# Seven half-depth block products in place of eight in the feed-forward gate and up projection

## The reference, cut to what matters

```python
h = _rmsnorm(x, norm_ffn_pre[l]).astype(dt)          # 1024 x 1024
gate, up = jnp.split(h @ ffn_w_up[l], 2, axis=-1)    # 1024 x 5632 -> 2 x 2816
gate = _causal_dwconv(gate, ffn_conv_w[l], ffn_conv_b[l])   # 3 taps
f = jax.nn.gelu(gate, approximate=True) * up
x = x + _rmsnorm(f @ ffn_w_down[l], norm_ffn_post[l]).astype(dt)
```

## Time and profile before

| | before |
|---|---|
| median of three runs | 3194.17 us |
| profiled execution, from its first to its last instruction (its own time) | 3201.0 us |
| TensorE busy | 2841.4 us (89%) |
| VectorE / ScalarE / GpSimd busy | 1815.1 / 1345.1 / 350.6 us |
| mean granted TensorE clock | 0.928 |

### The profile page before, as it was taken

The page is one execution under the profiler, slowest core; times in us unless marked ns, Lnnn a source line. Parts: engine busy times, 40 slices in busy tenths (PEclk is TensorE's granted clock), DMA queues, the critical chain, the costliest instruction groups (busy, mean ns, idle before and its releaser), DMA issues. The chain is left out here.

```text
span 3201.0 us, 42557 instructions
## 1 busy us (share of the span) xinstructions
PE 2841.4 (89%) x14715; PEld 2372.3 (74%) x14715; DVE 1815.1 (57%) x2267; ACT 1345.1 (42%) x2039; POOL 350.6 (11%) x246
## 2 busy tenths in 40 slices
PE   5999987799689999994999978677787999999998
PEld 5888776687578888883877777566676888887886
DVE  3995517764479999995462447664445233333344
ACT  4122427613178888883322134663335222222233
POOL 1222210020011112112122101002000000000000
PEclk9999998899789999997999978787598999999999
DMA  3112225133199999995212210402022111110122
GB/s 101 33 50 79 83 90 180 40 125 127 58 390 414 414 415 414 417 413 196 69 54 80 74 44 2 133 1 54 7 105 87 52 52 46 46 52 26 46 87 103
DMA packets 247664, 421.10 MB, mean 132 GB/s; under 512 B 33581, under 2 KB 152404, under 8 KB 247540
## 3 DMA queue, kind: packets, MB, share of 16 engines
q1 hardware_dynamic: 218356, 349.89, 30.3%
q10 hardware_dynamic: 20336, 39.59, 3.3%
q0 software_dynamic: 8848, 29.96, 2.8%
HBM read 349.05 MB, written 70.33 MB: 131 GB/s over the span
## 5 line engine op out<-in xcount | busy, mean ns | idle before, releaser
L2181 DVE TENSOR_TENSOR e_w_lo<-e_ring,e_w_hi 128x1024 fp32r<-128x1024 f32 x384 | 446.6, 1217 | 46.6 <-ACT e_w_hi L2108 46.6
L2108 ACT CAST e_w_hi<-e_ring 128x1024 fp32r<-128x1024 f32 x384 | 377.2, 1049 | 35.3 <-PE banks L2041 28.5
L2476 PE MATMUL banks<-h_hi,u_w_hi 128*128 128x512 f32 x672 | 262.8, 391 | 4.7 <-DVE u_w_lo L2519 4.7
L2477 PE MATMUL banks<-h_lo,u_w_hi 128*128 128x512 f32 x672 | 262.4, 391 | 0.0
L2478 PE MATMUL banks<-h_hi,u_w_lo 128*128 128x512 f32 x672 | 262.4, 390 | 0.0
L2039 PE MATMUL banks<-e_w_hi,e_xT_hi 128*128 128x512 f32 x512 | 203.1, 397 | 0.0
L2041 PE MATMUL banks<-e_w_hi,e_xT_lo 128*128 128x512 f32 x512 | 200.1, 391 | 0.0
L2040 PE MATMUL banks<-e_w_lo,e_xT_hi 128*128 128x512 f32 x512 | 199.7, 390 | 0.0
L949 DVE SCALAR_TENSOR_TENSOR conv<-x_first,vectors,conv 128x1024 f32<-128x1024 f32 x120 | 187.3, 1561 | 9.8 <-issue 0.9
L2476 PEld LDWEIGHTS banks<-h_hi,u_w_hi 128*128 128x128 f32 x672 | 126.8, 189 | 31.5 <-DVE u_w_lo L2519 4.9
L2296 PE MATMUL banks<-fd_w_hi,fd_s_hi 128*128 128x512 f32 x352 | 139.1, 395 | 11.4 <-DVE fd_s_lo L2392 11.4
(11 more groups left out here) (598 smaller groups left out, 6782.3 us busy)
## 6 DMA issues: line engine op xcount, KB each, us to landing
e_ring<-in_w_gate_e_dram SPq DMA_DIRECT2D x128, 512.0 KB, 6.0
e_ring<-in_w_up_e_dram SPq DMA_DIRECT2D x128, 512.0 KB, 6.1
e_ring<-in_w_down_e_dram SPq DMA_DIRECT2D x128, 512.0 KB, 5.2
yT<-in_ffn_w_up_dram SPq DMA_DIRECT2D x44, 512.0 KB, 3.9
expert_results<-nothing SPq DMA_DIRECT2D x1, 16384.0 KB
expert_results<-e_y ACTq DMA_DIRECT2D x32, 512.0 KB, 7.6
p_w<-in_w_in_dram SPq DMA_DIRECT2D x24, 512.0 KB, 3.8
fd_w<-in_ffn_w_down_dram SPq DMA_DIRECT2D x42, 256.0 KB, 2.6
```

Of the source, the lines that this page charges most:

```text
L2108: nc.scalar.copy(w_hi[:, part, :], experts.ring[:, slot, :]).then_inc(w_rounded, 1)
L2181: tt(w_lo[:, part, :], experts.ring[:, slot, :], w_hi[:, part, :].bitcast(F32), ALU.subtract).then_inc(w_split, 1)
L2476: nc.tensor.matmul(bank, w_hi[:, up, k, :], h_hi[:, k, tokens], start=(k == 0), stop=False)
L2477: nc.tensor.matmul(bank, w_hi[:, up, k, :], h_lo[:, k, tokens], start=False, stop=False)
```

## The change: what it does

**Products.** For column tile j let the gate weights be two halves of depth G0, G1 and the up weights U0, U1 (512 x 128 each), and let the activations be split by depth half and by token half: a0, a1 for tokens 0 to 511, b0, b1 for tokens 512 to 1023. Gate and up columns of both token halves are a 2 x 2 by 2 x 2 block product. It is made with seven products of half depth (4 depth slices, 512 tokens, 3 parts, so 12 matmuls each: 84 a tile) and not eight (96). The products are numbered m = 1 to 7. Products 1, 2 and 3 take plain activation halves (`own_hi`, `own_lo`), 4 to 7 take sums of them (`sum_hi`, `sum_lo`, which lie as four pieces of 128 tokens). Products 1, 2 and 4 take plain weights, 7, 5, 6 and 3 take weight sums. Their order for a tile is 1, 7, 5, 6, 2, 4, 3, apart from the first two tiles.

**Weight sums.** GpSimd makes four sums or differences of 128 x 512 for each tile (`weight_sums`), in two buffers. ScalarE and VectorE round and split seven operands of 128 x 512 a tile through a ring of five (before: two of 128 x 1024).

**Activation sums.** Before the loop, for each u of four, `chain(u)` on GpSimd (three operations of 128 x 512), `cross(u)` on VectorE (one), `round_sums(u)` on ScalarE and `part_sums(u)` on VectorE (128 x 2048 each). The products 1 and 2 of the first two tiles stand before them on TensorE; the first sums are used in two halves of 256 tokens.

**Combining.** ScalarE copies product 1 and the first gate half out of PSUM (128 x 512 each). VectorE does six additions of 128 x 512 with one operand in PSUM, in two of which an intermediate is formed.

**Result.** `f` is no longer kept in SBUF during `ffn_up`. Tiles 0 and 1 stay in `xn`; SP stores tiles 2 to 21 to DRAM (512 KB each), and `fd` loads them back while it makes its first pass. `ffn_up` ends only when the last store has landed. All streams of `ffn_up` are written out, without hardware loops.

```diff
-            with sp.Fori(1, pairs) as i:
-                for b in range(2):
-                    load(i, b, 0, i * 2 + b)
+            if rows is None:
...
+                for i in range(1, pairs):
+                    for b in range(2):
+                        sp.wait_ge(split, 4 * i + 2 * b + 1)
+                        sp.dma_start(w[:, b, :], weight[0][(2 * i + b) * P:(2 * i + b + 1) * P, 0:HALF]).then_inc(landed[b], 16)
+                    if i == 1:
+                        load_rows(1)
+                    if i + 1 < pairs:
+                        load_rows(i + 1)
...
-def ffn_up(K, h_hi, h_lo, room, f, norm, first, x_stored):
+def ffn_up(K, x, sums, xn, first, rows, x_stored):
...
+    KH, NH, RING = KT // 2, NT // 2, 5
+    order = [(0, 1), (0, 2), (1, 1), (1, 2)] + [(j, m) for j in range(2) for m in (7, 5, 6, 4, 3)] \
+        + [(j, m) for j in range(2, FFT) for m in (1, 7, 5, 6, 2, 4, 3)]
...
+            def store(j):
+                sp.wait_ge(done, j + 1)
+                sp.dma_start(rows[j * P:(j + 1) * P, :], c).then_inc(stored, 16)
...
+            sp.wait_ge(stored, 16 * (FFT - 2))
...
+                for k in range(KH):
+                    hi, lo = right(0, m, k, q), right(1, m, k, q)
+                    place = out if m in OWN else out.rearrange("p (u n) -> p u n", n=P)
+                    mm(place, w_hi[:, n % RING, k, :], hi, start=opens and k == 0 and not q, stop=False, skip_group_check=True)
+                    mm(place, w_hi[:, n % RING, k, :], lo, start=False, stop=False, skip_group_check=True)
+                    last = mm(place, w_lo[:, n % RING, k, :], hi, start=False, stop=(k == KH - 1), skip_group_check=True)
...
+            for t in range(4):
+                turn(t)
+            for m in (1, 2):
+                for q in range(2):
+                    pe.wait_ge(own_parted, 2 * q + 2)
+                    product(0, m, q)
+                    turn(2 * m + 2 + q)
+            product(1, 1)
+            product(1, 2)
+            for q in range(2):
+                pe.wait_ge(sum_parted, 2 * q + 2)
+                for m in (7, 5, 6):
+                    product(0, m, q)
...
+            def weight_sums(j):
+                pool.wait_ge(landed[j % 2], 32 * (j // 2) + 32)
+                if j >= 2:
+                    pool.wait_ge(split, at[j - 2, 3] + 1)
+                gate, upper, out = w[:, j % 2, 0], w[:, j % 2, 1], w_sums[j % 2]
+                tt(out[:, 0], gate[:, 0:KH], upper[:, 0:KH], ALU.subtract).then_inc(summed, 1)
+                tt(out[:, 1], upper[:, 0:KH], upper[:, KH:KT], ALU.add).then_inc(summed, 1)
+                pool.drain()
+                tt(out[:, 2], out[:, 1], gate[:, 0:KH], ALU.subtract).then_inc(summed, 1)
+                pool.drain()
+                tt(out[:, 3], gate[:, KH:KT], out[:, 2], ALU.subtract).then_inc(summed, 1)
...
+            def chain(u):
...
+                tt(tile_of(u)[:, low], tile_of(t)[:, low], tile_of(u)[:, low], ALU.subtract).then_inc(chained, 1)
...
+                pool.wait_ge(crossed, u + 1)
+                tt(tile_of(t)[:, high], tile_of(t)[:, high], tile_of(u)[:, low], ALU.subtract)
+                pool.drain()
+                tt(tile_of(u)[:, high], tile_of(u)[:, high], tile_of(t)[:, high], ALU.subtract).then_inc(chained, 1)
...
+            def event(n):
+                j, m = order[n]
+                if m == 7:
+                    dve.wait_ge(made, n + 1)
+                    dve.wait_ge(copied, j + 1)
+                    tt(xy, bank(j, 7), first[:, j % 2, :], ALU.add).then_inc(x_taken, 1)
+                if m == 5:
...
+                    tt(xy, bank(j, 5), xy, ALU.add).then_inc(y_taken, 1)
+                if m == 6:
+                    if j >= 1:
+                        finish(j - 1)
...
+                    tt(v, bank(j, 6), first[:, j % 2, :], ALU.add)
+                    tt(up[:, HALF:S], bank(j, 6), xy, ALU.add).then_inc(b_taken, 1)
+                if m == 4:
...
+                    tt(up[:, 0:HALF], bank(j, 4), v, ALU.add).then_inc(c_taken, 1)
+                if m == 3:
+                    dve.wait_ge(made, n + 1)
+                    tt(g[:, 2 + HALF:2 + S], bank(j, 3), v, ALU.add).then_inc(d_taken, 1)
+                fill(n + RING)
+                if m == 3:
+                    convolve(j)
...
+            for u in range(NH):
+                part_own(NH + u)
+                cross(u)
+                part_sums(u)
+                fill(5 + u)
...
+            f_rows = K.dram("ffn_rows", (DFF, S))
```

More of the change, by code:

```diff
@@ L2227, in _, with project_and_add @@
                 split_w(*tail(used, j))
-def project_and_add(K, tag, srcT, depth, weight, gain_row, x, y, src, out, squares=False, first=None):
+def project_and_add(K, tag, srcT, depth, weight, gain_row, x, y, src, out, squares=False, first=None, rows=None, head=None):
     nc = K.nc
@@ L2246, in project_and_add @@
     pairs = depth // 2
+    row_landed = [K.sem(f"{tag}_row_landed{b}") for b in range(2)] if rows is not None else None
     own = 16 if first is None else 0
@@ L2459, in _, with load @@
[L2459 to L2464, removed]
+            def load(j):
+                for up_half in range(2):
+                    sp.dma_start(w[:, j % 2, up_half], w_up[:, :, up_half * DFF + j * P:up_half * DFF + (j + 1) * P]).then_inc(landed[j % 2], 16)
@@ L2465, in _ @@
             sp.wait_ge(fetched, 32)
+            sp.wait_ge(stored, 16 * (FFT - 2))
         @block.tensor
         def _(pe):
[L2469 to L2486, removed]
+            mm = nc.tensor.matmul
+            def turn(t):
+                b = t % 2
+                pe.wait_ge(scaled, t + 1)
+                if t >= 2:
+                    pe.wait_ge(gained, t - 1)
+                for k in range(KT):
+                    last = nc.tensor.transpose(K.ps[:, 4 + 2 * b + k // 4, (k % 4) * P:(k % 4 + 1) * P], xn[:, b, k * P:(k + 1) * P], K.const("ident"))
+                last.then_inc(turned, 1)
@@ L2507, in _ @@
             act.wait_ge(rated, 1)
[L2508 to L2513, removed]
+            scale(0)
+            scale(1)
+            fill(0)
+            for t in range(NH):
+                round_own(t)
+                scale(t + 2)
+                if t < 3:
+                    fill(t + 1)
@@ new lines, in _ @@
+            for u in range(2):
+                scale(u + NT - 2)
+                round_own(NH + u)
+            event(0)
+            fill(4)
+            round_sums(0)
+            round_own(NH + 2)
+            event(2)
+            fill(5)
+            round_sums(1)
+            round_own(NH + 3)
+            fill(6)
+            round_sums(2)
+            fill(7)
+            round_sums(3)
+            fill(8)
+            for n in range(at[0, 7], len(order)):
+                event(n)
+            gelu(FFT - 1)
```

289 lines of the change are left out of this document (230 added, 59 removed).

## The result

The changed kernel takes 3174.8 us (median of four runs, 3169.7 to 3182.9) against 3194.9 us (3190.0 to 3201.1): ratio 0.9932, 95% interval 0.9915 to 0.9949, so 16 to 27 us are gained, 20.1 by the medians. The forecast was 3167. The profiled execution, the fastest of the four, has a span of 3167.9 us (before: 3201.0). The forecast's span for it was 3173.

A forecast was written before the change was run, and what follows sets the result against it. TensorE was taken as the bound, by matmul count and spacing. Start -37.3, end +8.6 and spacing +1 gave -27.7 us: 3194.2 to 3166.5, forecast 3167, own range 3157 to 3183, 8 in 10 3155 to 3189.

The forecast's parts named there:

- Bound and spacing: In the loop, TensorE is the bound at 0.2265 us a matmul; a tile falls from 21.7 to 19.0 us.
- rival B: In the loop, matmuls with a moving operand in four pieces run slower; gain gone at 26 ns each; chance 0.06.
- VectorE in the loop: Per loop tile, VectorE needs 14 us plus 3 for GpSimd's disturbance: 17 us, at most 18.6, under TensorE's 19.0.
- The 88%: Share of GpSimd's time that VectorE lost in an unbroken stretch of taps, 8.5 of 9.6 us; here at most 4.5 a tile.
- Rival A: In the loop, VectorE becomes the bound: strong form 22.0 us a tile, 3227, chance 0.07; mild 20 us, 3187, chance 0.08.
- ScalarE: Per loop tile, ScalarE's roundings, copies, gelu and at most two table loads take 9.3 us.
- The start: From the first scaling until TensorE's stream is unbroken, the longer preparation eats 22.5 of 59.8 us, leaving a gain of 37.3.
- 2448: In the start, the time in us by which plain rests of the first four tiles would be done.
- tiles 4 to 7 ... 3.7 us each: In the start, these tiles go one by one through 12 half matmuls, 8 transposes and a gain, reaching 2459.
- The end: From the last product to the first down-projection matmul, 12.9 us against 4.4 before: a loss of 8.6, between 6 and 12.
- rival D: In the down projection's first pass, row loads come late and each pair waits 1 us: 10 us more, 3177; chance 0.05.
- Rival C: In the start, rounds of sums take 13 us, not 9.4: 14 us more, 3181; chance 0.08.

The follow-up runs named there:

- experiment 5: Changed kernel with the four weight sums of tiles 2 to 21 on VectorE instead of GpSimd: 3173.62 us against 3196.05 for the kernel before.
- experiment 6: Changed kernel with each of GpSimd's weight sums made three times over: 3237.11 us against 3196.05 for the kernel before.
- Experiments 3: Changed kernel with VectorE's cross of the next round ahead of part_sums of this one: 3170.1 us, ratio 0.9914 to the kernel before.
- Experiment 2: Changed kernel with all eight turns of the norm ahead of TensorE's first products: 3165.98 us, ratio 0.991 to the kernel before.
- experiment 1: Kernel before, with one of eight depth slices left out of the products of tiles 1 to 21: 3142.9 us against 3197.05.
- the combined kernel: Changed kernel with turns first, activation sums on VectorE a round ahead and a shorter end: 3146.76 us; with weight sums on VectorE too, 3144.53.

## Why the prediction was right, step by step

**Bound and spacing: right.** 1848 matmuls, tiles 19.0 us apart (VectorE's L2778 at 2870.31 and 2889.31), no wait in the loop. B asked whether an operand in pieces is slower. Product 4 with its operand in four pieces and product 3 with a plain one follow each other in one spacing, 0.2265 us (2888.14, 2888.36, 2888.59, 2888.82, 2889.04, 2889.27, the last two on the plain operand); rival B is dead.

```profile
2888.82 0.39 PE L2585 MATMUL banks<-u_sums,u_w_lo 128*128 128x512 f32 x1
2889.04 0.39 PE L2583 MATMUL banks<-u_own_hi,u_w_hi 128*128 128x512 f32 x1
```

**VectorE in the loop: right in kind, over-sized.** "So I take 3: 17 us of VectorE a tile" measured 14.1. GpSimd's disturbance is 0.9 us a tile, not 3, and without it VectorE has 13.2 and not 14: four of seven rests are 0.2 us longer (913 and 893 against 689 to 693), and the taps (1.28) and PSUM additions (0.68 to 0.69) not at all. The 88% of the earlier trace rows came from a stretch in which VectorE never paused and read SBUF only. Here most of GpSimd's 6.0 us a tile (131.1 us of its eight groups over 22 tiles) falls beside VectorE's PSUM additions and its idle time: some 30 of its 47 us between 2600 and 2750. Rival A's condition wasn't met: in experiment 5 VectorE has 15.6 us of work a tile, 3.4 less than TensorE, and TensorE never waits. Its price stays untested. That experiment 6 comes to the same 22.0 us a tile is chance: rival A reached it with one set of weight sums and 0.25 us at each of 14 waits, experiment 6 with three sets, and there GpSimd is the bound. Nor does it bear out the 88%. VectorE's busy time rises from 14.1 to 20.3 us a tile (92% of 22.0) for 8 x 1.29 = 10.3 us more of GpSimd's work, 60%, and GpSimd's own twelve operations are stretched from 17.1 to 22.0 us.

The Trainium skill (page SBUF — State Buffer, section on the two separate sides) says that a VectorE operation with two SBUF inputs, or in a mode that uses both of its ports, and a GpSimd operation that reads SBUF exclude each other for a whole instruction. Experiments 3 and 6 agree, down to the PSUM additions that escape it. The first tap (TENSOR_SCALAR) has a single SBUF tensor as input and is doubled too; no run shows in which mode it worked. The 19.2 us a tile that the prediction made of the rule, by adding up busy times, were too many against 14.1: the exclusion costs only where the two meet.

**ScalarE: over-sized.** 125.7 us in 380 are 6.3 us a tile, not 9.3. Seven roundings and two copies at 0.63 and a gelu at 1.05 are 6.7 us; "at most two table loads at 1.28" were not there: one table load in the whole written-out stage, where the hardware loop before had twenty. Nothing hung on it.

**The start: the step that was under-sized.** On the way to 2448 the prediction slips: 2432.3, 4 x 3.1 and 1.5 make 2446.2. The plain rests were done 20.1 us after the first scaling, for 18.9 by its 2448 and 17.1 by its terms; two weight rests took 1.20 and 1.75 us for 0.69 beside GpSimd's first weight sums. Forecast from the first scaling to the last split sum 67.2 us, measured 70.5. The rounds were forecast at 9.4 and took 8.9, a little in favour; what failed most is "tiles 4 to 7 ... 3.7 us each". From the end of the last plain rest (2439.94) to the end of tile 7's gain (2454.74) 14.8 us passed for what had been put at 11, with idle times of 3.50, 5.94 and 1.69 us. Experiment 2 takes the half matmuls out from between and gains 9.2. The 36 half matmuls behind the sums took 7.0 us for 6 (2490.39 to 2497.34): 27 and not 16 of them came every 0.21 us. TensorE's whole stretch from the first scaling to its end is 477.5 us (2419.82 to 2897.36) for a forecast 472.7 + 1: 3.8 us too many, 3.3 of them up to the last split sum and 1.0 in those half matmuls, less 0.5 in the loop. Of the ideal 57.3 us (experiment 1) the start took 24.9 and the end 8.3.

**The end: right.** 12.8 us (12.78 in the row) for a forecast 12.9. **The down projection: right.** Its first matmul's wait apart, TensorE stood 7.0 us for `fd_s_lo` before (L2296: 11.4 - 4.4) and 7.0 after (L2317: 19.8 - 12.8): the loads of the rows of `f` are hidden; rival D is dead. Rival C (13 us a round) too.

**The sum.** Forecast -27.7, local -24.1 from the terms above. The medians gave -20.1 and -21.8, and both intervals (-16 to -27, and -18 to -27) hold the local value. Over all eleven comparisons the medians say from 1.4 us more to 5.6 us less gain than the local totals, 2.1 less on average. Where those 2 us lie is open. It isn't the down projection, which takes 257.2 to 258.6 us in all twelve traces; the spread of the stages ahead of the first scaling hides them.

**Where the expected gain went,** then: more than half of the 57 us that fewer products are worth was paid for preparing the sums in a chain over three engines while TensorE waits at a low clock (24.9) and for a bare end (8.3). 27.8 of these 33.3 come back with another order of the same work and VectorE in GpSimd's place; in the combined kernel the start costs 2.0 us more than in experiment 1 and the end 3.4.

## What to carry to other kernels

A scheme that trades products for sums gains in the loop what the matmul spacing says, as long as no other engine needs more than that for a tile; its costs lie where the sums of the shared operand must be ready before the first product that uses them, so write out that chain engine by engine before the loop, put nothing ahead of it on any queue, and keep it on one engine if its operations are short. Work given to GpSimd beside VectorE is worth pricing by where the two meet: close to nothing beside PSUM operations and pauses, 60 to 88% of its duration in the two saturated stretches seen here (experiment 6 and the earlier trace rows), and all of it in a serial chain. When a profiled span and the medians disagree by more than the effect looked for, count between two events that enclose the change and nothing else.

## What the runs showed of the hardware that was not expected

- VectorE additions with one operand in PSUM are untouched by GpSimd even at its 93% (692 ns), while operations that read only SBUF take 1.7 to 2 times as long: 693 to 1307, 813 to 1602, 1285 to 2153 ns.
- GpSimd's 128x512 operations go from 1.29 us alone to 3.31 when caught behind VectorE's 2.29 us one.
- A matmul's moving operand in four separate runs of 128 tokens costs nothing against one run of 512: 0.2265 us from matmul to matmul with either.
- The granted clock in the start is 0.69 with TensorE idle half the time, and 1.00 in the loop with an unbroken stream.
- The written-out stage has one activation table load of 1.28 us; the hardware loop of before had 20 around the same two functions.
